# A first feed-forward tile ahead of its norm's root, and four slots for split weights, in a two-block transformer kernel

## What is computed

```python
def conv_ffn(x_n, w_up, conv_w, w_down):              # first model, twice
    g, u = jnp.split(causal_dwconv(x_n @ w_up, conv_w), 2, axis=-1)
    return (jax.nn.silu(g) * u) @ w_down
# layer 0: h += short_conv_mixer(rms_norm(h)); h += conv_ffn(rms_norm(h)); shared latent keys and values
# layer 1: h += mla_attention(rms_norm(h), ...); h += conv_ffn(rms_norm(h)); h = rms_norm(h, final)
# second model, one layer, with six modulation vectors (shift, scale, gate, twice) from c @ w_ada + b_ada:
#   x += (1 + gate1) * mixer(rmsnorm(x) * (1 + scale1) + shift1)   # gating, stick-breaking, dilated windows
#   h  = rmsnorm(x, g_ffn) * (1 + scale2) + shift2                 # the norm that the change is about
#   x += (1 + gate2) * (silu(conv(h @ w_up)[:2816]) * conv(h @ w_up)[2816:]) @ w_down
#   return rmsnorm(x, g_final)
```

## Time and profile before

| | us |
|---|---|
| median of 3 runs | 1749.2 |
| lowest, highest | 1746.62, 1749.9 |
| the profiled execution, its own time | 1745.34 |
| its span in the trace | 1743.6 |
| TensorE busy | 1718.7 (99%) |
| VectorE busy | 1136.1 (65%) |
| ScalarE busy | 698.6 (40%) |
| GpSimd busy | 394.0 (23%) |
| mean DMA rate | 107 GB/s |

### The profile page before, as it was taken

How to read it: one execution, slowest core, us unless ns; L and a number is a source line. 1 busy time by engine, 2 the same in 40 slices (tenths; PEclk the granted TensorE clock), 3 DMA queues, 4 the chain that set the end, 5 groups by cost and what they waited for, 6 DMA issues and landing times.

```text
span 1743.6 us, 22081 instructions
## 1 busy us (share of the span) xinstructions
PE 1718.7 (99%) x7877; PEld 1397.9 (80%) x7877; DVE 1136.1 (65%) x1429; ACT 698.6 (40%) x952; POOL 394.0 (23%) x169
## 2 busy tenths in 40 slices
PE   9999999999999999999999999999999999999998
PEld 6888788888887878878888888888657788888886
DVE  7566777776656796677777666563765677777222
ACT  4123444444333556444444422432563544444221
POOL 2444100000544440310000055544202200000442
PEclk9999999999999999999999999999999999999999
DMA  5232222333664220133222366432201222222331
GB/s 195 98 107 99 90 98 96 96 98 113 231 217 145 85 97 1 61 109 96 96 96 96 120 218 217 144 101 85 73 1 50 83 97 96 96 96 96 97 109 73
DMA packets 52188, 186.34 MB, mean 107 GB/s; under 512 B 5920, under 2 KB 6048, under 8 KB 52128
## 3 DMA queue, kind: packets, MB, share of 16 engines
q1 hardware_dynamic: 51552, 184.34, 31.7%
q10 hardware_dynamic: 576, 1.20, 0.2%
HBM read 183.41 MB, written 2.10 MB: 106 GB/s over the span
## 4 chain that ended last, share of the span: by engine, by line
PE 91%; DVE 4%; ACT 3%; issue 1%; POOL 0%; DMA 0%; DVEq 0%; ACTq 0%; SPq 0%
PE ps L1596 27%; PE ps L1598 27%; PE ps L1597 27%; PE ps L1903 1%; PE ps L1781 1%; PE ps L1782 1%; PE ps L1783 1%; DVE acc L974 1%; PE ps L1892 1%; PE ps L1641 0%; PE ps L2014 0%; PE ps L1981 0%; PE ps L1636 0%; DMA X<-x_in 0%; PE ps L1655 0%
## 5 line engine op out<-in xcount | busy, mean ns | idle before, releaser
L525 POOL TENSOR_TENSOR WL<-raw,WH 128x1024 fp32r<-128x1024 f32 x156 | 382.9, 2454 | 1317.5 <-ACT WH L570 1317.5
L1596 PE MATMUL ps<-XH,WH 128*128 128x512 f32 x1480 | 579.4, 391 | 2.5 <-DVE XL L1370 1.0
L1598 PE MATMUL ps<-XH,WL 128*128 128x512 f32 x1480 | 576.0, 389 | 0.0
L1597 PE MATMUL ps<-XL,WH 128*128 128x512 f32 x1480 | 575.9, 389 | 0.0
L570 ACT ACTIVATE WH<-raw 128x1024 fp32r<-128x1024 f32 x291 | 308.3, 1060 | 533.2 <-PE ps L1598 501.5
L1596 PEld LDWEIGHTS ps<-XH,WH 128*128 128x128 f32 x1480 | 277.9, 188 | 64.1 <-issue 3.5
L1597 PEld LDWEIGHTS ps<-XL,WH 128*128 128x128 f32 x1480 | 277.9, 188 | 58.1 <-issue 1.0
L1598 PEld LDWEIGHTS ps<-XH,WL 128*128 128x128 f32 x1480 | 277.8, 188 | 58.0
L1596 PE MATMUL ps<-HH,WH 128*128 128x512 f32 x528 | 205.6, 389 | 0.1
L1598 PE MATMUL ps<-HH,WL 128*128 128x512 f32 x528 | 205.4, 389 | 0.0
L1597 PE MATMUL ps<-HL,WH 128*128 128x512 f32 x528 | 205.4, 389 | 0.0
(11 more groups left out here) (298 smaller groups left out, 2001.8 us busy)
## 6 DMA issues: line engine op xcount, KB each, us to landing
raw<-w_tiles SPq DMA_DIRECT2D x291, 512.0 KB, 3.3
ada<-ada_tiles SPq DMA_DIRECT2D x32, 512.0 KB, 5.5
trig<-ada_tiles SPq DMA_DIRECT2D x16, 512.0 KB, 6.7
X<-x_in SPq DMA_DIRECT2D x4, 512.0 KB, 6.6
out_x<-X SPq DMA_DIRECT2D x8, 256.0 KB, 2.0
RAB<-c_in SPq DMA_DIRECT2D x2, 512.0 KB, 4.5
MK<-mask_in ACTq DMA_DIRECT2D x1, 640.0 KB, 3.8
trig<-rope_in SPq DMA_DIRECT2D x2, 256.0 KB, 2.8
```

The lines of the kernel that those rows point to most:

```text
L525: nc.gpsimd.tensor_tensor(WL[k % SPL][:, :], raw[:, k, :], f32(WH[k % SPL][:, :]), ALU.subtract).then_inc(s_lo, 1)
L1596: mm(bank, h, xh, start=first, stop=False)
L1597: mm(bank, h, xl, start=False, stop=False)
L1598: return mm(bank, lo, xh, start=False, stop=last)
```

## The change

- `SPL` is 4: high and low halves are made four tiles ahead, and the 4 + 4 slots take another 16 KB on each partition (the DMA scratch of the program is made smaller for it). VectorE's share of the low halves moves two tiles later in each up product, and OUT2's third tile goes to GpSimd.
- For N_F2 the residual stage also makes `QXH` and `QXL`, the halves of X times the gain (g_ffn and scale2), without the root. `ahead_of_root` multiplies UP2's first tile by them, with the sum of squares after its third chunk and the spread after its fourth. Beside it 16 matmuls of two columns give the shift's product in `ps[6]`. The eviction of that tile multiplies by `rb` and adds the reduced shift. `two_tiles` now takes tiles 1 and 2. The mask matmuls here go.
- At the start, the high halves of tiles 2 and 3 are made among the squares, without a wait for TensorE.
- In UQ the rope bank of the last pair comes one place earlier than its heads would have it: the order of banks is r0 h0 h1 r1 h2 h3 r2 h4 r3 h5 h6 h7, on all engines. ScalarE's high parts of the last rope move into the attention (after block 4), VectorE's low parts of the last two after blocks 4 and 8. The table of the exponential is loaded before the first query head, the table of the root before OUT2's residual stage.

```diff
@@ -47,7 +47,7 @@
 BLK = 8
 TILE = BLK * P
 RAW = 4
-SPL = 2
+SPL = 4
 ADA = 3
 CONV = 3
 
...
@@ -111,7 +111,6 @@
     own = {0, 1}
     for name in ("UP0", "UP1", "UP2"):
         own |= set(range(t0[name] + SPL, t0[name] + SPL + 2 * FF))
-    own |= {t0["OUT2"] + 2}
     return own
 
 
...
@@ -358,7 +363,7 @@
         NORM_CHUNKS = [KD, KD, KD, KKV, KQ, KD, KD, KD, KD]
         N_A, N_F0, N_KV, N_LK, N_LQ, N_F1, N_FIN, N_F2, N_END = range(9)
         SQ0 = [sum(NORM_CHUNKS[:i]) for i in range(10)]
-        APART = (N_FIN, N_F2, N_END)
+        APART = (N_FIN, N_END)
         ACC0 = [sum(NORM_CHUNKS[:i]) - sum(n < i for n in APART) for i in range(10)]
         E_A, E_F0, E_KV, E_Q, E_F1, E_M2, E_F2 = range(7)
 
...
@@ -607,7 +614,7 @@
                 def body(i):
                     for k in range(4):
                         m = i * 4 + k
-                        late = n in APART and m == KD - 1
+                        late = n >= N_FIN and m == KD - 1
                         for j in range(tiles_per_m - late):
                             ahead(T0[phase] + k * tiles_per_m + j, i, per)
                         act.wait_ge(s_acc, m + (ACC0[n] - 1))
...
@@ -617,6 +624,9 @@
                             nc.scalar.activation(at(XH, m), at(X, m), ACT.Copy, scale=vcol(gname, m))\
                                 .then_inc(s_xh, 1)
                         nc.scalar.activation(SQ[:, k % 2, :], at(X, m), ACT.Square).then_inc(s_sq, 1)
+                        if n == N_F2:
+                            nc.scalar.activation(QXH[:, m, :], X[:, m, :], ACT.Copy, scale=gm[:, 1, m:m + 1])\
+                                .then_inc(s_gxh, 1)
                         if second:
                             act.wait_ge(s_acc2, m + 1)
                             apart()
...
@@ -679,8 +689,8 @@
                 if m >= 2:
                     act.wait_ge(s_acc, m - 1)
                 nc.scalar.activation(SQ[:, m % 2, :], X[:, m, :], ACT.Square).then_inc(s_sq, 1)
-                if m == 1:
-                    ahead(T0["A_CH"])
+                if m == 1 or m == 3:
+                    hi(2 + m // 2)
             act.wait_ge(s_set, 1)
             act.wait_ge(s_in["vec"], 16)
 
...
@@ -689,8 +699,7 @@
                 for k in range(4):
                     if isinstance(i, int) and k == 2:
                         root(N_A, D, rb)
-                    if not isinstance(i, int) or k > 0:
-                        ahead(T0["A_CH"] + k, i, 4)
+                    ahead(T0["A_CH"] + k, i, 4)
             repeat(act, 4, a_ch, peel=1)
 
             def a_b(i):
...
@@ -826,6 +835,8 @@
                     half_hi(a // 4 - 2)
                 block_exp(a + 1)
                 block_norm(a)
+                if a == 4:
+                    rope_hi(3)
             block_norm(BLOCKS_A - 1)
             half_hi(HEADS - 2)
             half_hi(HEADS - 1)
...
@@ -947,6 +958,7 @@
                     window_norm(u)
             class_hi(2)
             class_hi(3)
+            nc.scalar.preload_act_table(ACT.Sqrt)
             residual("OUT2", 1, None, N_F2)
 
             token_root(N_F2)
...
@@ -1031,19 +1043,19 @@
                                 gm[:, gate, :][:, bass.ds(m, 1)]
                             ins = v.scalar_tensor_tensor(at(X, m), bank, g, at(X, m), ALU.mult, ALU.add)
                         ins.then_inc(s_ev, 1)
-                        if phase == "OUT2" and m == 0:
-                            low(T0["OUT2"] + 2, 0)
                         if gname:
                             lo_half(at(XH, m), at(XL, m), at(X, m), vcol(gname, m), (s_xh, m + (KD * e + 1)), s_xl)
                         if n in APART and m == KD - 1:
                             early_sums(n)
                             continue
                         add_square(n, m, k)
+                        if n == N_F2:
+                            lo_half(QXH[:, m, :], QXL[:, m, :], X[:, m, :], gm[:, 1, m:m + 1], (s_gxh, m + 1), s_gxl)
                         if second:
                             dve.wait_ge(s_sq2, m + 1)
                             dve.wait_ge(s_acc2, m + 2)
                             v.tensor_tensor(rbl[:, :], rbl[:, :], AT[:, k % 2, :], ALU.add).then_inc(s_acc2, 1)
-                repeat(dve, KD // 4, body, peel=KD // 4 if n in APART else KD // 4 if phase == "WO" else 0)
+                repeat(dve, KD // 4, body, peel=KD // 4 if n >= N_FIN or phase == "WO" else 0)
 
             def conv(dst, src, w, j, chunks, last):
 
...
@@ -1065,7 +1077,13 @@
 
                 def evict(M, i, pad):
                     product(M, i, 4)
-                    if deferred:
+                    if M == M0["UP2"] and isinstance(i, int):
+                        dve.wait_ge(s_moved, 1)
+                        v.reduce_sum(epsc[:, 1:2], ps[6][:, 0:2], AX_X).then_inc(s_first, 1)
+                        v.tensor_tensor(pad[:, 2:S + 2], ps[M % 4][:, :], rb[:, :], ALU.mult).then_inc(s_first, 1)
+                        dve.wait_ge(s_first, 2)
+                        ins = v.tensor_scalar(pad[:, 2:S + 2], pad[:, 2:S + 2], epsc[:, 1:2], None, ALU.add)
+                    elif deferred:
                         ins = v.tensor_tensor(pad[:, 2:S + 2], ps[M % 4][:, :], rb[:, :], ALU.mult)
                     else:
                         ins = v.tensor_copy(pad[:, 2:S + 2], ps[M % 4][:, :])
...
@@ -1371,6 +1403,8 @@
                                                mod[:, shift * KD + k:shift * KD + k + 1], f32(XH[:, k, :]),
                                                ALU.add, ALU.subtract).then_inc(s_xl, 1)
             modulated(E_M2, NB_M2, 0, 0, ps[4])
+            ch.link(v.tensor_copy(shift[:, :, 0], mod[:, 3 * KD:4 * KD]))
+            v.tensor_tensor(shift[:, :, 1], mod[:, 3 * KD:4 * KD], f32(shift[:, :, 0]), ALU.subtract).then_inc(s_shift, 1)
             dve.wait_ge(s_bc, 3)
 
             def first_result(m):
...
@@ -1560,10 +1594,10 @@
             residual("OUT2", 1, None, None, N_F2, gate=2)
 
 
-            whole_sums(N_F2)
             token_inverse(N_F2)
             dve.wait_ge(s_bc, 4)
             modulated(E_F2, NB_F2, 1, 3, ps[4])
+            ch.link(v.tensor_copy(rb[:, :], ps[4][:, :]))
             ch.link(v.memset(acc[:, :], 0.0))
             up(2, "UP2", False)
             residual("DN2", 3, None, None, N_END, gate=3)
...
@@ -1623,6 +1657,25 @@
                     last = dot(ps[(M + j) % 4][:, :], t + j, k, XH[:, k, :], XL[:, k, :], k == 0, k == KD - 1)
                     if k == KD - 1:
                         last.then_inc(s_pe, 1)
+
+            def ahead_of_root(t, M, n):
+
+                bank_free(M)
+                pe.wait_ge(s_shift, 1)
+                for k in range(KD):
+                    for w in (WH, WL):
+                        move = mm(ps[6][:, 0:2], w[t % SPL][:, k * P:(k + 1) * P], shift[:, k, :],
+                                  start=k == 0 and w is WH, stop=k == KD - 1 and w is WL)
+                    if k == KD - 1:
+                        move.then_inc(s_moved, 1)
+                    pe.wait_ge(s_gxl, k + 1)
+                    last = dot(ps[M % 4][:, :], t, k, QXH[:, k, :], QXL[:, k, :], k == 0, k == KD - 1)
+                    if k == 2:
+                        pe.wait_ge(s_acc, ACC0[n + 1])
+                        token_squares(acc, 0)
+                    if k == 3:
+                        spread(3, ps[4], 4)
+                last.then_inc(s_pe, 1)
 
             def inputs(e):
 
...
@@ -1733,9 +1786,11 @@
                             tile_ready(T0[phase] + k)
                         else:
                             tile_ready(T0[phase] + 4 + k, i - 1, 4)
-                        if start and n is None and k < 2:
+                        if start and f == 2 and k < 3:
                             if k == 0:
-                                two_tiles(T0[phase], M0[phase], inputs(e))
+                                ahead_of_root(T0[phase], M0[phase], n)
+                            if k == 1:
+                                two_tiles(T0[phase] + 1, M0[phase] + 1, inputs(e))
                             continue
                         wide(T0[phase] + k, M0[phase] + k, i, 4, inputs(e) if start and k == 0 else None, ready=False,
                              within=n if start and k == 0 else None)
...
@@ -2125,15 +2180,7 @@
 
             for m in range(2, KD):
                 wide(T0["OUT2"] + m, M0["OUT2"] + m)
-            pe.wait_ge(s_acc, ACC0[N_F2 + 1])
-            token_squares(acc, 0, ps[5], s_early)
-            awake(5)
-            pe.wait_ge(s_sq, SQ0[N_F2 + 1])
-            token_squares(SQ[:, 1, :], 0)
-            awake(5)
-            spread(3, ps[4], 4)
-            awake(9)
-            up(2, "UP2", E_F2, None)
+            up(2, "UP2", E_F2, N_F2)
             down(2, "DN2")
             pe.wait_ge(s_acc, ACC0[N_END + 1])
             token_squares(acc, 0, ps[5], s_early)
...
```

## The result

The changed kernel takes 1740.16 us (median of five runs, 1737.81 to 1740.24) against 1749.2 for the kernel before (1746.62 to 1751.71 in five): a ratio of 0.995, interval 0.9939 to 0.9961. It is 9.0 us faster; 4.4 were forecast, and the time lies just under the range. The profiled execution took 1740.24 us.

A forecast was written before the change was run, and what follows sets the result against it. TensorE, busy 1718.7 of 1743.6 us, was taken as the bound. Terms of -4.9 - 0.9 + 1.3 + 1.5 - 1.0 gave -4.0, with bubbles -4.4, so 1749.2 became 1744.8; range 1740.5 to 1748.8 for 8 in 10.

The forecast's parts named there:

- part 4: Queries and attention: 2.4 us gained at the first transposes, 1.4 given back by inserted rope parts; net gain 1.0.
- -4.9 - 0.9 + 1.3 + 1.5 - 1.0: In order: UP2's first tile, low-half waits, the sum's wait at DKV, the start, queries and attention; -4.0 us together.
- Offset: Profiled execution 3.9 us below the median of the runs; the difference was carried unchanged to the forecast.
- Part 1: Between OUT2 and UP2: first up tile runs ahead of the root, gaining 4.9 us (3.4 to 5.4).
- Part 2: Four slots: low-half waits at IN2's and OUT2's third tiles go, gaining 0.9 us; DKV loses 1.3.
- the bubbles: Short TensorE waits of 0.1 to 0.3 us at the third up tiles; -0.4 added to the sum.
- DKV's loss: After the last down product, a raw tile behind the rotation tables delays the sum; 1.3 us lost (1.0 to 2.5).
- Part 3: The start: earlier splits of tiles 2 and 3 delay sums, root and first eviction; 1.5 us lost.
- GpSimd's lock: At the start, GpSimd's split stops VectorE's sums through a shared port pair; without this rule the start costs 0.4 us.
- ScalarE's queue stands: Slower rival, chance 0.07: ScalarE waits in order for raw tiles over 8 us late together; 1753 us.
- Attention takes it back: Rival, chance 0.24: rope parts inserted between attention blocks cost 4.1 us in place of 1.4; 1747.5 us.
- The prices stay hidden: Rival, chance 0.24: start and DKV cost nothing, so the change gains 7.2 us; 1742.0 us.

The follow-up runs named there:

- b_again: The kernel before, unchanged, run and profiled a second time: 1748.2 us, ratio 0.9992.
- v_attn3: The changed kernel with queries, rope parts and the exponential's table as before: 1743.87 us, ratio 0.9977 to the kernel before.
- b_table3: The kernel before with only the exponential's table loaded early, ahead of the first query head: 1746.23 us, ratio 0.9993.
- b_awake3: The kernel before with nine unread mask matmuls ahead of the attention's first transposes: 1747.18 us, ratio 0.9991.
- v_first: The changed kernel with UP2's first tile put back behind the root: 1744.12 us, ratio 0.9976 to the kernel before.
- v_rope: The changed kernel with both rotation tables loaded three raw tiles later: 1738.72 us, ratio 0.9943 to the kernel before.
- v_start: The changed kernel with the start's high halves made as before: 1739.36 us, ratio 0.9944 to the kernel before.
- v_both3: The changed kernel with the start as before and the rotation tables three raw tiles later: 1736.21 us, ratio 0.9933 to the kernel before.

## Why the prediction was too small

The mechanisms were there one by one, and none of the rivals was the case. The time was missed by 4.6 us (9.0 against 4.4). Taken as the traces stand, 3.9 of that is the offset between the profiled executions and the medians, and 0.7 the sum (5.1 in the spans). But the two profiled executions had different luck with the clock. At equal clock the change is worth 6.8, so 2.2 of the miss is clock and 2.4 is the sum. Two steps failed.

The first is this sentence: *"The profiled execution lies 3.9 below the median of the runs, so I carry the difference."* The difference wasn't a constant of the measurement. The execution that was profiled was of the quickest kind, at a clock of 0.998, and most others run at 0.993 to 0.997. One place that sets them apart is the very gap that part 4 closes: behind TensorE's 1.88 us the clock fell in two of the three traces that have it in full (`b_again`, `v_attn3`), for 2.5 and 2.3 us, and in `b_table3` right behind 1.27. The profiled execution paid none of this, so its trace couldn't show it; the median pays, and the change removes it. The kernel after lies 0.1 from its profiled execution.

The second is the size of the terms in *"-4.9 - 0.9 + 1.3 + 1.5 - 1.0"*: every gain but that at the transposes was put too low and every price too high, by 3.1 in all, as the points below give. (The norm ahead of IN2 is why that is more than 2.4: it lost 0.7 in `v_attn3`, with a low stretch no longer than before, and as much in `b_awake3`, which has none of the change.)

Point by point:

- *Offset* (the change of the medians less that of the profiled executions; 0 expected, -3.9 found): 2.2 of it is the mean clock, which the change raises (9.0 less the 6.8 at equal clock). The other 1.7 is that the two profiled executions weren't alike. The one after lost 0.5 by the first product and had the longer low stretch at IN2's norm. `b_again` lost 0.5 and 1.2 at the same two places with no edit, so I take this part for chance; no run separates it.
- *Part 1* (4.9 forecast, 5.5 in the traces): sums, spread and the 2-column matmuls cost what was taken, and the edit is 4.6. Wrong was *"is worth nothing by itself"* of the root's table: `v_first` leaves 0.9 for it, since the load stood in the chain that TensorE waited for.
- *Part 2*: the third tiles of IN2 and OUT2 gained 1.5 where 0.9 was taken; the bubbles gained 1.1 where 0.4 was taken. DKV's loss was 0.9, from the named mechanism, where 1.3 was taken (bounds 1.0 to 2.5); `v_rope` takes it back.
- *Part 3*: 1.4 for 1.5, with GpSimd's lock in both places. The recorded step adds up to 1.2 rather than 1.5: 33.3, the eviction's end, less 32.1, when the bank was wanted.
- *Part 4*: the gain of 2.4 is there (2.3). The price of the inserted rope parts was 0.7, where 1.4 was taken (0.5 to 3): TensorE waited for little of them. Without the clock the part is worth 1.7 in the traces, where 1.0 was forecast; with it 3.7 or more.
- The slower rival, *ScalarE's queue stands*, needed raw tiles 8 us late. In the changed kernel one was 0.9 late; where TensorE came earlier (`v_start`) the sum was 2.7 later than it needed to be, with the clock behind it. The mechanism exists, at a third of the size.
- *Attention takes it back* was weighed at 0.24 and is refuted by 0.7. *The prices stay hidden* (7.2 in the spans) comes near the 6.8 at equal clock for the wrong reason: the prices of the start and of DKV were paid, 1.4 and 0.9.

Left open: how much of the kernel before's 3.9 comes from the attention alone. Filling its gap gave 1.4, closing it 3.7 with the 1.7 of its own included, and neither interval is narrow enough to share out the rest among the start, DN0, IN2's norm and UP2.

## What to carry to other kernels

A profiled execution is one draw. Before its times are carried to a median, compare its mean granted clock with that of the other executions, and where it is at the top, look in the trace for gaps of TensorE like the one of 1.88 us here, which could have cost clock and happened not to. In this kernel an edit that closes such a gap is worth what it saves in waiting, plus some 2 us in the executions where the clock fell. But filling one gap isn't sure to pay: in `b_awake3`'s trace the clock fell at another place instead. And a gain made ahead of a late transfer comes to an end at that transfer: move both, as `v_both3` did, or neither.

## What the runs showed of the hardware

- Behind the same wait of 1.88 us the granted clock stayed at 2.4 GHz in one execution and went to 1.2 GHz for some 7 us in two others, for 2.5 and 2.3 us of loss. Behind a wait of 1.27 it fell for some 3 us. With waits of 3.42 and 3.01 it fell in both traces.
- In the norm ahead of IN2 it falls in each of the twelve traces, for some 3 us or some 7, though TensorE is busy with narrow matmuls there; that moved the end by 1.2 us between two traces of one kernel.
- ScalarE's load of a table takes 1.28 us and its next instruction starts 1.30 us after the load's start; where a root stood behind it with TensorE waiting, loading it earlier gained 0.9.
- Eight pairs of 2-column matmuls, each with its own weight load, stretch the stream by 0.24 us a pair.
- From 0.993 to 0.998 of mean clock the kernel before becomes 5.8 us faster (1751.2 to 1745.4), about 1.2 us for each 0.001.
